# Rotary pairs swapped by transfers and copies instead of products in a three-layer hybrid block

## The chip, the core and the metric

The kernel runs on one core of a Trainium2 chip. Its engines work side by side, each through its own queue in order: TensorE (PE) for products, VectorE (DVE) and ScalarE (ACT) for work on tiles, GpSimd (POOL), and SyncE (SP), which here only issues the weights' transfers. They wait for each other through semaphores. The metric is the time of one execution in microseconds (us), measured on the device.

## What is computed

One sequence of 256 tokens with 1024 features goes through three layers, each a mixer and a gated feed-forward part (2816 wide), all in float32. The first layer mixes an RG-LRU, a gated linear attention and a block attention. The other two, which the change touches, mix an RWKV-7 recurrence, a dilated attention (B) and a latent attention (C):

```python
def rope_tables(positions, dim):
    inv_freq = 1.0 / (ROPE_THETA ** (jnp.arange(0, dim, 2, dtype=jnp.float32) / dim))
    ang = positions.astype(jnp.float32)[..., None] * inv_freq
    return jnp.cos(ang), jnp.sin(ang)

def apply_rope(t, cos, sin):
    t1, t2 = jnp.split(t, 2, axis=-1)
    c = cos[:, :, None, :].astype(t.dtype)
    s = sin[:, :, None, :].astype(t.dtype)
    return jnp.concatenate([t1 * c - t2 * s, t1 * s + t2 * c], axis=-1)

def partial_rope(t, cos, sin):
    rot, rest = jnp.split(t, [B_ROT_DIM], axis=-1)
    return jnp.concatenate([apply_rope(rot, cos, sin), rest], axis=-1)
...
    q = partial_rope(q, cos, sin)
    k = partial_rope(k, cos, sin)
...
    q = (rms_norm_2(cq, q_norm_g) @ w_uq).reshape(bsz, seq, C_HEADS, C_NOPE_DIM + C_ROPE_DIM)
    kv = (rms_norm_2(ckv, kv_norm_g) @ w_ukv).reshape(bsz, seq, C_HEADS, C_NOPE_DIM + C_V_DIM)
...
    q_rope = apply_rope(q_rope, cos, sin)
    k_rope = apply_rope(k_rope[:, :, None, :], cos, sin)[:, :, 0]
```

The first two calls are the dilated mixer's, on 16 of the 64 features of each of four heads (`B_ROT_DIM`); the last two are the latent mixer's, on 64 features of each query head and on one key that its four heads share. A rotation needs each feature beside its partner: 8 features away in B's heads, 32 in C's.

## The kernel before

Features lie on the 128 partitions and tokens along them, so a tile of two heads is 128 x 256. A feature's partner is on another partition.

Each float32 product is made of three: operands are split into a high part (`hi`, by ACT) and a rest (`lo`, by DVE), and `product` (line 466) runs hi by hi, lo by hi and hi by lo. The weights come in chunks of up to 1 MB through a ring of three buffers (`raw`, `w_hi`, `w_lo`): SP's queue loads a chunk, ACT writes `w_hi` (`hi_of`, line 1207), DVE `w_lo` (`lo_of`, line 1676). The order of all work on each engine is written out by hand; a step that others wait for is marked by name (`V.mark`, `A.mark`, `M.mark`) and awaited by that name.

In an RWKV layer (`rwkv(l)` on each engine) the recurrence needs the inverses of eight triangular 128 x 128 blocks, which are built up in levels n = 1 to 5 and a joining step 6. A level is: PE's first products (`inv_y`, line 937); ACT's copy of them (`inverse_y`); PE's back products (lines 921 and 926); DVE's subtractions from `x` and `xt` (line 1658), which the next level's first products wait for, half by half. DVE also makes masks for the level after (`level`, line 2158). Between and beside these steps each engine has `beside_inverse(n, half)`: half 0 stands behind the first products, half 1 behind the back products (on DVE: ahead of and behind the subtractions). What stands there:

- PE: at level 1 the projection of `bv` (chunk `in` 8, between the steps); at (2, 0) the products with `rot_b` for B's queries `bq` and keys `bk`, then `up(0)`; `up(1)`, `up(2)` at (2, 1), (3, 0); at (3, 1) the products with `dup` and `dup_rot`, which double C's shared rotary key `krope` from 64 to 128 partitions, plain and swapped, then `up(3)`; `up(4)` at (4, 0); at (4, 1) the product with `rot_c` for C's rotary queries `qr`; at (5, 0) the first attention scores; `up(5)`. `up(i)` are the products of the normed latents (`cq`, `ckv`) with `uq` and `ukv`.
- DVE: `rotate(n, dst, v, swapped, cos)` multiplies a tile by the cosine, its swapped copy by the sine and adds them: three operations. It rotates `bq`, `bk`, `krope` and `qr` at (2, 0), (3, 0), (3, 1) and (4, 1). `latents_lo` writes the latents' rests at (1, 1), behind it the evacuation of `bv` (line 1761), which `up(0)` waits for.
- ACT: copies of the latents into `h_hi` at level 1, copies of each `up(i)` (line 1451), and splits of chunks.

`cq_hi` and `cq_lo` are the first three tiles of `h_hi` and `h_lo`, which the projections read as their input until the last of them, that of `bv`, is done. So the copy waits for it (`act.wait_ge(M.sem, M.at(l, "in", 8))`). The swap matrices are constants with a sign in them, and the product's output stays in PSUM (banks 6 and 7).

Of the kernel before, what the change touches and what calls it, by code (L numbers as in the profile page):

```python
# [36 lines left out]
P = 128  # L37
# [96 lines left out]
def constants():  # L134
    i = np.arange(P)
    freq = np.zeros((P, 4), np.float32)
# [5 lines left out]
    freq[:, 2], freq[:, 3] = EPS, 64e-5  # L142

# [22 lines left out]
    rb, rc = np.zeros((P, P)), np.zeros((P, P))  # L166
    for h in (0, 64):
        for j in range(8):
            rb[h + j + 8, h + j], rb[h + j, h + j + 8] = -1, 1
        for j in range(32):  # L170
            rc[h + j + 32, h + j], rc[h + j, h + j + 32] = -1, 1
    dup = np.zeros((P, P))
    dup[i % 64, i] = 1
    out |= {"rot_b": rb, "rot_c": rc, "dup": dup}
    dupr = np.zeros((P, P))
    dupr[:64] = rc[:64, :64] @ dup[:64]
    out["dup_rot"] = dupr
# [49 lines left out]
def program(nc, ins, out, plan):  # L227


    with ExitStack() as ctx:  # L230
# [21 lines left out]
        rstd_col = sb("rstd_col", [P, TT])  # L252
        ARENA = 18752
        arena = sb("arena", [P, ARENA])
        bank = [ctx.enter_context(nc.psum_tensor(f"bank{i}", [P, 512], F32)) for i in range(8)]
# [70 lines left out]
        cq_hi, cq_lo = h_hi[:, 0:3, :], h_lo[:, 0:3, :]  # L326
        small = sb("small", [P, 96])
        filler = rope[:, 0, :]
# [15 lines left out]
        stored = sem("output_stored")  # L344
        V = Steps(sem("vector_step"), plan.get("V"))
# [100 lines left out]
        def _(pool):  # L446
# [13 lines left out]
        def _(pe):  # L460
# [602 lines left out]
            def up(l, i):  # L1063
# [8 lines left out]
                if i == 5:  # L1072
                    pe.wait_ge(V.sem, V.at(l, "rotated", 3))
# [13 lines left out]
            def beside_inverse(l, n, half):  # L1087


                b = AT2  # L1090
                if (n, half) == (2, 0):
                    pe.wait_ge(V.sem, V.at(l, "in", 7))
                    pe.wait_ge(A.sem, A.at(l, "rkv"))
                    pe.wait_ge(A.sem, A.at(l, "kb_turned"))
                    pe.matmul(bank[6][:, :], C("rot_b"), B2["bq"].rearrange("p a b -> p (a b)"), start=True, stop=True)
                    pe.matmul(bank[7][:, :], C("rot_b"), B2["bk"].rearrange("p a b -> p (a b)"), start=True, stop=True)\
                        .then_inc(M.sem, M.mark(l, "b_rot"))
# [7 lines left out]
                if (n, half) == (3, 1):  # L1105
                    pe.wait_ge(V.sem, V.at(l, "rotated", 0))
                    pe.matmul(bank[6][:, 0:T], C("dup")[0:64, :], B2["krope"][0:64, :], start=True, stop=True)
                    pe.matmul(bank[6][:, T:2 * T], C("dup_rot")[0:64, :], B2["krope"][0:64, :], start=True, stop=True)\
                        .then_inc(M.sem, M.mark(l, "k_rot"))
# [3 lines left out]
                if (n, half) == (4, 1):  # L1113
                    pe.wait_ge(V.sem, V.at(l, "rotated", 1))
                    pe.matmul(bank[7][:, :], C("rot_c"), b["qr"].rearrange("p a b -> p (a b)"), start=True, stop=True)\
                        .then_inc(M.sem, M.mark(l, "q_rot"))
# [86 lines left out]
        def _(act):  # L1203
# [105 lines left out]
            def ffn(l):  # L1309
# [21 lines left out]
                for p in range(1, FT // 2):  # L1331
# [4 lines left out]
                    if l == 0 and p == 6:  # L1336

                        act.wait_ge(V.sem, V.at("angles"))
                        for i in range(4):
                            last = act.activation(rope[:, i, :], rope[:, i, :], ACT.Sin)  # L1340
# [83 lines left out]
            def rwkv(l):  # L1424
# [6 lines left out]
                def beside_inverse(n):  # L1431
                    if n == 1:
                        hi_of(CHUNK[l, "ukv", 0])
                        act.wait_ge(M.sem, M.at(l, "in", 8))
# [1059 lines left out]
```

## Time and profile before

| | |
|---|---|
| median of 3 runs | 1014.27 us (1014.16 to 1014.28) |
| the profiled execution | 1013.86 us, span in the trace 1012.1 us |
| PE busy | 98% |
| DVE, ACT, POOL busy | 68%, 50%, 0% |
| granted TensorE clock | 0.999 |
| transfers | 156.41 MB, mean 155 GB/s |

The span runs from the first to the last instruction in the trace; the time of an execution is a little longer. Busy PE includes products that overlap, so a share of 98% says that it hardly ever waits, not that it is at its peak.

### The profile page before, as it was taken

The numbers are of one execution on the slowest core, as the hardware profiler recorded it, in microseconds if no ns is written. First come the engines' busy times: TensorE is split into PE (matmuls) and PEld (weight loads), VectorE is DVE, ScalarE is ACT, GpSimd is POOL, SyncE is SP. The second block draws the span as 40 slices with busy tenths as digits, with TensorE's granted clock in tenths as the row PEclk, the third lists the DMA queues.
The fourth block names the chain that finished last, engine by engine and source line by source line (L and its number), as shares of the span: only waits on it lengthen the run. The fifth ranks groups of instructions, "written<-read, shape, count | busy, mean of one in ns | idle before, by whom it ended". The sixth has DMA issues, their size and how long they took to land.

```text
span 1012.1 us, 20189 instructions
## 1 busy us (share of the span) xinstructions
PE 996.9 (98%) x8762; PEld 948.7 (94%) x8762; DVE 684.5 (68%) x1093; ACT 501.2 (50%) x667; POOL 3.0 (0%) x8
## 2 busy tenths in 40 slices
PE   9999999999999999999999999999999999999997
PEld 8898999999999889889999999999887999999997
DVE  6868586785656897856665565588877566565555
ACT  6466664435345652645544434375436364434433
POOL 0000000000000000000000000000000000000000
PEclk9999999999999999999999999999999999999999
DMA  9535345455544332314454545543231254555531
GB/s 332 179 113 200 138 147 190 173 209 186 189 170 159 109 111 85 124 46 141 167 208 174 196 173 180 196 161 116 79 111 44 89 203 170 189 184 173 202 126 42
DMA packets 24024, 156.41 MB, mean 155 GB/s; under 512 B 2608, under 2 KB 3936, under 8 KB 6400
## 3 DMA queue, kind: packets, MB, share of 16 engines
q1 hardware_dynamic: 21888, 151.70, 41.7%
q10 hardware_dynamic: 1840, 2.50, 0.7%
q8 instruction: 69, 1.13, 0.4%
q0 software_dynamic: 208, 0.92, 0.3%
q14 instruction: 19, 0.16, 0.0%
HBM read 154.05 MB, written 1.06 MB: 153 GB/s over the span
## 4 chain that ended last, share of the span: by engine, by line
PE 87%; DVE 6%; ACT 3%; issue 2%; DMA 1%; SPq 0%; ACTq 0%; DVEq 0%
PE bank L466 73%; DVE w_lo L1676 2%; ACT w_hi L1207 2%; DVE arena L1658 1%; PE bank L921 1%; PE bank L926 1%; PE bank L937 1%; DVE x L1658 1%; DMA x<-in_x 1%; PE bank L1145 1%; PE bank L1175 1%; DVE arena L2150 1%; DVE h_lo L1690 0%; ACT h_hi L1251 0%; PE bank L884 0%
## 5 line engine op out<-in xcount | busy, mean ns | idle before, releaser
L466 PE MATMUL bank<-h_hi,w_hi 128*128 128x256 f32 x1480 | 424.3, 287 | 3.7 <-DVE arena L1770 1.5
L1676 DVE TENSOR_TENSOR w_lo<-raw,w_hi 128x2048 fp32r<-128x2048 f32 (+2 forms) x142 | 318.7, 2250 | 155.9 <-ACT w_hi L1207 155.3
L466 PE MATMUL bank<-h_lo,w_hi 128*128 128x256 f32 x1480 | 418.7, 283 | 0.0
L466 PE MATMUL bank<-h_hi,w_lo 128*128 128x256 f32 x1480 | 418.6, 283 | 0.0
L1207 ACT ACTIVATE w_hi<-raw 128x2048 fp32r<-128x2048 f32 (+2 forms) x151 | 271.3, 1801 | 77.1 <-PE bank L466 74.9
L466 PEld LDWEIGHTS bank<-h_hi,w_hi 128*128 128x128 f32 x1480 | 283.6, 192 | 11.0 <-issue 4.9
L466 PEld LDWEIGHTS bank<-h_lo,w_hi 128*128 128x128 f32 x1480 | 283.7, 192 | 1.0 <-issue 0.7
L466 PEld LDWEIGHTS bank<-h_hi,w_lo 128*128 128x128 f32 x1480 | 283.7, 192 | 0.0
L466 PE MATMUL bank<-mix_hi,w_hi 128*128 128x256 f32 x720 | 207.0, 287 | 2.2 <-DVE mix_lo L1658 1.4
L466 PE MATMUL bank<-mix_lo,w_hi 128*128 128x256 f32 x720 | 203.7, 283 | 0.0
L466 PE MATMUL bank<-mix_hi,w_lo 128*128 128x256 f32 x720 | 203.7, 283 | 0.0
L466 PEld LDWEIGHTS bank<-mix_hi,w_hi 128*128 128x128 f32 x720 | 138.1, 192 | 5.1 <-DVE mix_lo L1658 2.3
L466 PEld LDWEIGHTS bank<-mix_lo,w_hi 128*128 128x128 f32 x720 | 138.1, 192 | 1.0 <-issue 1.0
L466 PEld LDWEIGHTS bank<-mix_hi,w_lo 128*128 128x128 f32 x720 | 138.1, 192 | 0.0
L1321 ACT ACTIVATE arena<-arena 128x256 f32<-128x256 f32 x66 | 27.6, 418 | 194.9 <-DVE arena L1658 194.9
L1658 DVE TENSOR_TENSOR arena<-arena 128x256 f32<-128x256 f32 (+2 forms) x134 | 71.6, 541 | 47.5 <-ACT arena L1321 35.3
L1207 ACT ACTIVATE arena<-bank 128x256 f32<-128x256 f32 (+3 forms) x72 | 30.9, 448 | 49.8 <-PE bank L603 17.2
L1658 DVE TENSOR_TENSOR mix_lo<-arena,mix_hi 128x256 fp32r<-128x256 f32 (+1 forms) x70 | 30.8, 441 | 33.3 <-ACT mix_hi L1207 33.3
L1207 ACT ACTIVATE mix_hi<-arena 128x256 fp32r<-128x256 f32 (+1 forms) x70 | 30.1, 430 | 38.5 <-DVE arena L1658 37.3
L1658 DVE TENSOR_TENSOR arena<-bank,rstd 128x512 f32<-128x512 f32 x66 | 45.1, 684 | 0.0
L466 PE MATMUL bank<-w_hi,h_hi 128*128 128x256 f32 (+1 forms) x84 | 25.7, 306 | 0.0
L1258 ACT ACTIVATE h_hi<-x,par 128x256 fp32r<-128x256 f32 x32 | 14.1, 500 | 22.6 <-DVE x L1658 16.5
(310 smaller groups left out, 844.3 us busy)
## 6 DMA issues: line engine op xcount, KB each, us to landing
raw<-in_w SPq DMA_DIRECT2D x136, 1024.0 KB, 4.8
raw<-in_w SPq DMA_DIRECT2D x5, 512.0 KB, 3.9
raw<-in_w SPq DMA_DIRECT2D x2, 896.0 KB, 4.4
raw<-in_w SPq DMA_DIRECT2D x2, 768.0 KB, 4.7
cst<-in_consts SPq DMA_DIRECT2D x1, 1184.0 KB, 10.6
arena<-bias_rows ACTq DMA_DIRECT2D x1, 1024.0 KB, 7.3
out<-arena ACTq DMA_DIRECT2D x4, 256.0 KB, 2.1
mat<-in_mat POOLq DMA_DIRECT2D x2, 384.0 KB, 3.4
```

The source lines that it names most:

```text
L466: last = pe.matmul(dst, w[a](k), act[b](k), start=start and i == 0 and j == 0, stop=stop and i == n - 1 and j == 2, skip_group_check=loose)
L921: last = pe.matmul(blocks(quads(2 + q)[h, m % 4, 0:64], n, 1), Y[h, m, :], blocks(XT[h, m, :], n, 1), start=True, stop=True)
L926: last = pe.matmul(blocks(quads(q)[h, m % 4, 0:64], n, 0), XT[h, m, :], blocks(Y[h, m, :], n, 0), start=True, stop=True)
L937: last = pe.matmul(quads(q)[h, m % 4, 0:64], BT[h, m, :], Xm[h, m, :], start=True, stop=True)
L1145: pe.matmul(dst(i), AT2["qn"][:, i - 4, queries], AT2["kn"][:, i - 4, keys], start=True, stop=False)
L1175: pe.matmul(dst(j), value(j, 0), att_p(l, j)[:, 0:T], start=True, stop=False)
L1207: return act.activation(dst, src, ACT.Copy, **kw)
L1258: last = act.activation(h_hi[:, k, :], x[:, k, :], ACT.Copy, scale=Par(g, k))
L1321: act.activation(FF["sg"][:, j % 2, :], FF["gu"][:, j % 2, 0, :], ACT.Silu)\
L1658: ins_ = dve.tensor_tensor(dst, a, b, op)
L1676: dve.tensor_tensor(w_lo[:, s, 0:n], raw[:, s, 0:n], w_hi[:, s, 0:n].bitcast(F32), ALU.subtract)\
L2150: last = dve.copy_predicated(gram[:, g, 2 * n:2 * n + 2, :].rearrange("p a b -> p (a b)"), mask, pairs(g % 4)[:, n, :])
```

## The change

The swap is no longer a product with a matrix. B's queries and keys: POOL issues four transfers each (8 partitions, two tiles of 256 columns, 16 KB) that move the partner features of two heads into another tile, `SWAP`. C's key: POOL copies it to the upper 64 partitions, then four copies of 32 partitions. C's queries: ACT writes the swapped tile with four more copies out of `up(2)`'s bank. The sign now sits in the sine tables, through a scale of -1 or 1 by partition in the sine (`freq`'s two new columns). The latents' parts lie in memory of their own, `latents`, over tiles of the area that are used later (`rs`, `nsa`, `s1`, `y`); so ACT's copy no longer waits for the last projection, and the memset of `s1` moves behind `up(2)`. The rotations stand one step sooner. DVE's split of chunk `out` 0 moves from (4, 0) to (3, 1), ACT's of `out` 1 behind `up(4)`.

```diff
+    freq[:, 4], freq[:, 5] = np.where(i % 16 < 8, -1, 1), np.where(i % 64 < 32, -1, 1)
...
+        latents = nc.alloc_sbuf_tensor_at("latents", [P, 2, 3, T], F32R, offset=arena_at + 29 * T * 4)
...
+        SWAP = dict(bq=B2["pm"][:, 0:2, :], bk=B2["pm"][:, 2:4, :], k=B2["pm"][:, 4, :], q=s_hl[:, 6:8, :])
+        HALF_PAIRS = [(slice(h + a, h + a + 32), slice(h + 32 - a, h + 64 - a)) for h in (0, 64) for a in (0, 32)]
+        cq_hi, cq_lo = latents[:, 0, :, :], latents[:, 1, :, :]
...
             for l in range(LAYERS):
+                if l:
+                    pool.wait_ge(V.sem, V.at(l, "kr"))
+                    for n, (dst, src) in enumerate(
+                            [(B2["krope"][64:P, :], B2["krope"][0:64, :])] +
+                            [(SWAP["k"][to, :], B2["krope"][from_.start % 64:from_.start % 64 + 32, :])
+                             for to, from_ in HALF_PAIRS]):
+                        if n:
+                            pool.wait_ge(k_swapped, 5 * l - 5 + n)
+                        pool.tensor_scalar(dst, src, 1.0, 0.0, ALU.mult, ALU.add).then_inc(k_swapped, 1)
+                    pool.wait_ge(M.sem, M.at(l, "gate"))
+                    for name, i in (("bq", 6), ("bk", 7)):
+                        pool.wait_ge(V.sem, V.at(l, "in", i))
+                        for h in (0, 64):
+                            for a in (0, 8):
+                                pool.dma_start(SWAP[name][h + a:h + a + 8, :, :],
+                                               B2[name][h + 8 - a:h + 16 - a, :, :]).then_inc(b_swapped[name], 16)
...
                 if (n, half) == (2, 0):
-                    pe.matmul(bank[6][:, :], C("rot_b"), B2["bq"].rearrange("p a b -> p (a b)"), start=True, stop=True)
-                    pe.matmul(bank[7][:, :], C("rot_b"), B2["bk"].rearrange("p a b -> p (a b)"), start=True, stop=True)\
-                        .then_inc(M.sem, M.mark(l, "b_rot"))
...
                 if (n, half) == (3, 1):
-                    pe.wait_ge(V.sem, V.at(l, "rotated", 0))
-                    pe.matmul(bank[6][:, 0:T], C("dup")[0:64, :], B2["krope"][0:64, :], start=True, stop=True)
-                    pe.matmul(bank[6][:, T:2 * T], C("dup_rot")[0:64, :], B2["krope"][0:64, :], start=True, stop=True)\
-                        .then_inc(M.sem, M.mark(l, "k_rot"))
                     up(l, 3)
...
-                if (n, half) == (4, 1):
-                    pe.wait_ge(V.sem, V.at(l, "rotated", 1))
-                    pe.matmul(bank[7][:, :], C("rot_c"), b["qr"].rearrange("p a b -> p (a b)"), start=True, stop=True)\
-                        .then_inc(M.sem, M.mark(l, "q_rot"))
...
                         hi_of(CHUNK[l, "ukv", 0])
-                        act.wait_ge(M.sem, M.at(l, "in", 8))
                         act.wait_ge(V.sem, V.at(l, "c_n"))
...
                         up(i)
-                        if i == 2:
+                        if i == 4:
                             hi_of(CHUNK[l, "out", 1])
...
+                    last = act.activation(up_to[i], up_bank(i), ACT.Copy, scale=scale if i < 3 else 1.0)
+                    if i == 2:
+                        for to, from_ in HALF_PAIRS:
+                            last = act.activation(SWAP["q"][to, :, :], up_bank(i)[from_, :, :], ACT.Copy, scale=scale)
+                    last.then_inc(A.sem, A.mark(l, "up", i))
...
                     if (n, half) == (1, 1):
                         latents_lo()
+                        dve.wait_ge(b_swapped["bq"], 64 * l)
+                        rotate(0, B2["bq"], B2["bq"], SWAP["bq"], 0)
                         evacuate(l, 8, B2["bv"], token_major=True)
-                    if (n, half) == (2, 0):
-                        after_m(l, "b_rot")
-                        rotate(0, B2["bq"], B2["bq"], pairs(6), 0)
                     if (n, half) == (2, 1):
                         lo_of(CHUNK[l, "ukv", 0])
+                    if (n, half) == (2, 0):
+                        dve.wait_ge(b_swapped["bk"], 64 * l)
+                        rotate(1, B2["bk"], B2["bk"], SWAP["bk"], 0)
                     if (n, half) == (3, 0):
-                        rotate(1, B2["bk"], B2["bk"], pairs(7), 0)
+                        dve.wait_ge(k_swapped, 5 * l)
+                        rotate(2, b["kro"], B2["krope"], SWAP["k"], 2)
                     if (n, half) == (3, 1):
-                        after_m(l, "k_rot")
-                        rotate(2, b["kro"], bank[6][:, 0:T], bank[6][:, T:2 * T], 2)
+                        lo_of(CHUNK[l, "out", 0])
                     if (n, half) == (4, 0):
-                        lo_of(CHUNK[l, "out", 0])
+                        after_a(l, "up", 2)
+                        rotate(3, b["qr"], b["qr"], SWAP["q"], 2)
+                        dve.nop().then_inc(V.sem, V.mark(l, "c_rope"))
                     if (n, half) == (4, 1):
-                        after_a(l, "up", 2)
-                        after_m(l, "q_rot")
-                        rotate(3, b["qr"], b["qr"], pairs(7), 2)
-                        dve.nop().then_inc(V.sem, V.mark(l, "c_rope"))
+                        after_m(l, "up", 2)
+                        dve.memset(B2["s1"].rearrange("p a b -> p (a b)"), 0.0)
```

The order on DVE, from the last subtraction of level 1 to the first of level 2, before (`h_lo` takes the latents' rests, `rstd_col` marks the evacuation of `bv`, `cst` the level masks, `rope` the tables):

```order
L1658 TENSOR_TENSOR arena<-arena,bank3 128x64x2
L1658 TENSOR_TENSOR h_lo<-spare_49,h_hi 128x512
L1658 TENSOR_TENSOR h_lo<-spare_49,h_hi 128x256
L1761 TENSOR_SCALAR arena<-bank4,rstd_col 128x256 x2
L2158 TENSOR_TENSOR arena<-arena,cst 128x256 x2
L1658 TENSOR_TENSOR spare_49<-arena,rope 128x512
L1658 TENSOR_TENSOR spare_49<-bank6,rope 128x512
L1658 TENSOR_TENSOR arena<-spare_49 128x512
L1658 TENSOR_TENSOR arena<-arena,bank0 128x32x4
```

and in the changed kernel:

```order
L1662 TENSOR_TENSOR arena<-arena,bank3 128x64x2
L1662 TENSOR_TENSOR latents_50<-spare_49,latents_50 128x512
L1662 TENSOR_TENSOR latents_50<-spare_49,latents_50 128x256
L1662 TENSOR_TENSOR spare_49<-arena,rope 128x512 x2
L1662 TENSOR_TENSOR arena<-spare_49 128x512
L1765 TENSOR_SCALAR arena<-bank4,rstd_col 128x256 x2
L2163 TENSOR_TENSOR arena<-arena,cst 128x256 x2
L1662 TENSOR_TENSOR spare_49<-arena,rope 128x512 x2
L1662 TENSOR_TENSOR arena<-spare_49 128x512
L1662 TENSOR_TENSOR arena<-arena,bank0 128x32x4
```

The rotation of `bq` has moved ahead of the evacuation, and that of `bk` has taken its place behind the masks; neither reads a bank.

The order on DVE from the last subtraction of level 3 to the first of level 4, before (`w_lo` is the split of chunk `out` 0):

```order
L1658 TENSOR_TENSOR arena<-arena,bank3 128x16x8
L1658 TENSOR_TENSOR spare_49<-bank6,rope 128x256 x2
L1658 TENSOR_TENSOR spare_49<-spare_49 128x256
L2158 TENSOR_TENSOR arena<-arena,cst 128x256 x2
L1676 TENSOR_TENSOR w_lo<-raw,w_hi 128x2048
L1658 TENSOR_TENSOR arena<-arena,bank0 128x8x16
```

and in the changed kernel, where the row ahead of the first subtraction is now the sum of `qr`'s rotation:

```order
L1662 TENSOR_TENSOR arena<-arena,bank3 128x16x8
L1680 TENSOR_TENSOR w_lo<-raw,w_hi 128x2048
L2163 TENSOR_TENSOR arena<-arena,cst 128x256 x2
L1662 TENSOR_TENSOR spare_49<-spare_49,rope 128x512 x2
L1662 TENSOR_TENSOR spare_49<-spare_49 128x512
L1662 TENSOR_TENSOR arena<-arena,bank0 128x8x16
```

The rotation of `krope` has left this stretch, that of `qr` has come in, and the split stands ahead of the masks.

The order on ACT from the copies of `up(0)` and `up(1)` on, before:

```order
L1451 ACTIVATE spare<-bank 128x512 x2
L1207 ACTIVATE w_hi<-raw 128x2048
L1207 ACTIVATE arena<-bank 128x256 x2
L1451 ACTIVATE spare<-bank 128x512
L1207 ACTIVATE w_hi<-raw 128x2048
L1451 ACTIVATE spare<-bank 128x512
L1207 ACTIVATE arena<-bank 128x256 x2
L1451 ACTIVATE spare<-bank 128x512
```

and in the changed kernel:

```order
L1452 ACTIVATE spare<-bank 128x512 x2
L1208 ACTIVATE w_hi<-raw 128x2048
L1208 ACTIVATE arena<-bank 128x256 x2
L1452 ACTIVATE spare<-bank 128x512
L1455 ACTIVATE spare<-bank 32x512 x4
L1452 ACTIVATE spare<-bank 128x512
L1208 ACTIVATE arena<-bank 128x256 x2
L1452 ACTIVATE spare<-bank 128x512
```

Behind `up(2)` stand four copies of 32 partitions instead of a `w_hi` split, which has moved behind `up(4)`.

## Rows read from the trace of the kernel before

**Rows 1.** The page, busy time of each engine and its share of the span

```profile
PE 996.9 (98%) x8762; PEld 948.7 (94%) x8762; DVE 684.5 (68%) x1093; ACT 501.2 (50%) x667; POOL 3.0 (0%) x8
```

**Rows 2.** The page, the chain that ended last, by engine

```profile
PE 87%; DVE 6%; ACT 3%; issue 2%; DMA 1%; SPq 0%; ACTq 0%; DVEq 0%
```

**Rows 3.** Line 1095 (`rot_b` by `bq`): ns min/median/max, first and last start

```profile
L1095 PE MATMUL bank<-arena,cst x4: 592/644/697, 398.4 to 737.5; 128*128 128x512 f32 x4
```

**Rows 4.** Timeline of PE, layer 1: start us, us, engine line

```profile
398.39 1.13 PE L1095 MATMUL bank<-arena,cst 128*128 128x512 f32 x2
...
400.42 0.36 PE L466 MATMUL bank<-h_hi,w_hi 128*128 128x256 f32 x1
...
408.47 0.66 PE L921 MATMUL bank<-arena 64*64 64x32 f32 x16
...
410.45 0.70 PE L1107 MATMUL bank<-arena,cst 64*128 64x256 f32 x2
...
411.51 0.39 PE L466 MATMUL bank<-h_hi,w_hi 128*128 128x256 f32 x1
...
412.41 1.15 PE L937 MATMUL bank<-arena 64*64 64x64 f32 x32
...
416.39 1.13 PE L1115 MATMUL bank<-spare,cst 128*128 128x512 f32 x2
417.44 1.15 PE L937 MATMUL bank<-arena 64*64 64x64 f32 x32
```

**Rows 5.** Timeline of DVE, layer 1; in brackets its idle time before, and the releaser

```profile
375.73 5.42 DVE L2150 COPY_PREDICATED arena<-cst,bank 128x256 f32<-128x256 uint32 x16 [0.80 <-PE bank L884]
...
388.21 0.69 DVE L1770 TENSOR_TENSOR arena<-bank,rstd 128x512 f32<-128x512 f32 x1 [0.82 <-PE bank L466]
...
394.36 0.49 DVE L1658 TENSOR_TENSOR arena<-arena,bank 128x128 f32<-128x128 f32 x2 [0.45 <-PE bank L926]
398.38 1.03 DVE L1658 TENSOR_TENSOR h_lo<-spare,h_hi 128x512 fp32r<-128x512 f32 x2 [3.54 <-ACT h_hi L1207]
399.45 0.88 DVE L1761 TENSOR_SCALAR arena<-bank,rstd_col 128x256 f32<-128x256 f32 x2
...
400.91 0.68 DVE L1658 TENSOR_TENSOR spare<-arena,rope 128x512 f32<-128x512 f32 x1
...
402.23 0.69 DVE L1658 TENSOR_TENSOR arena<-spare 128x512 f32<-128x512 f32 x1
...
410.57 0.49 DVE L1658 TENSOR_TENSOR arena<-arena,bank 128x128 f32<-128x128 f32 x2 [0.37 <-PE bank L926]
...
412.40 0.43 DVE L1658 TENSOR_TENSOR spare<-spare 128x256 f32<-128x256 f32 x1
413.22 0.82 DVE L2158 TENSOR_TENSOR arena<-arena,cst 128x256 f32<-128x256 f32 x2 [0.39 <-PE bank L937]
413.95 2.28 DVE L1676 TENSOR_TENSOR w_lo<-raw,w_hi 128x2048 fp32r<-128x2048 f32 x1
416.16 1.11 DVE L1658 TENSOR_TENSOR arena<-arena,bank 128x128 f32<-128x128 f32 x4
```

**Rows 6.** Timeline of ACT, layer 1; in brackets its idle time before, and the releaser

```profile
397.42 0.94 ACT L1207 ACTIVATE h_hi<-spare 128x512 fp32r<-128x512 f32 x2 [6.78 <-PE bank L466]
...
406.24 1.91 ACT L1207 ACTIVATE w_hi<-raw 128x2048 fp32r<-128x2048 f32 x1
408.04 0.65 ACT L1207 ACTIVATE arena<-bank 128x256 f32<-128x256 f32 x2
408.56 0.61 ACT L1451 ACTIVATE spare<-bank 128x512 f32<-128x512 f32 x1
```

**Rows 7.** Lines 448 and 453 on POOL: ns min/median/max, starts; its transfers' landing

```profile
L448 POOL TENSOR_SCALAR w_hi<-raw x1: 1038/1038/1038, 5.8 to 5.8; 128x1024 fp32r<-128x1024 f32 x1
...
L453 POOL DMA_DIRECT2D mat<-in_mat x2: 538/624/709, 114.4 to 461.7; - x2
...
DMA to landing us min/median/max: 3.3/3.4/3.6
```

More of the change, by code:

```diff
@@ L135, in constants @@
     i = np.arange(P)
-    freq = np.zeros((P, 4), np.float32)
+    freq = np.zeros((P, 6), np.float32)
     for h in (0, 64):
@@ L164, in constants @@
     out["dilated"] = np.where((dist >= 0) & (count > 0), np.log(np.maximum(count, 1)), NEG)
[L166 to L177, printed above, removed]
     return {k: np.asarray(v, np.float32) for k, v in out.items()}
@@ L251, in program @@
         rstd = sb("rstd", [P, T])
-        rstd_col = sb("rstd_col", [P, TT])
         ARENA = 18752
+        arena_at = nc.sbuf_base
         arena = sb("arena", [P, ARENA])
+        latents = nc.alloc_sbuf_tensor_at("latents", [P, 2, 3, T], F32R, offset=arena_at + 29 * T * 4)
         bank = [ctx.enter_context(nc.psum_tensor(f"bank{i}", [P, 512], F32)) for i in range(8)]
@@ L325, in program @@
             [B2[name].rearrange("p a b -> p (a b)")[:, 0:384] for name in ("kkn", "kp")]
-        cq_hi, cq_lo = h_hi[:, 0:3, :], h_lo[:, 0:3, :]
+        SWAP = dict(bq=B2["pm"][:, 0:2, :], bk=B2["pm"][:, 2:4, :], k=B2["pm"][:, 4, :], q=s_hl[:, 6:8, :])
+        HALF_PAIRS = [(slice(h + a, h + a + 32), slice(h + 32 - a, h + 64 - a)) for h in (0, 64) for a in (0, 32)]
+        cq_hi, cq_lo = latents[:, 0, :, :], latents[:, 1, :, :]
         small = sb("small", [P, 96])
+        rstd_col = sb("rstd_col", [P, TT])
         filler = rope[:, 0, :]
@@ L344, in program @@
         stored = sem("output_stored")
+        k_swapped = sem("k_rope_swapped_by_gpsimd")
+        b_swapped = {name: sem(f"{name}_pairs_swapped") for name in ("bq", "bk")}
         V = Steps(sem("vector_step"), plan.get("V"))
@@ L1071, in up @@
                     pe.wait_ge(A.sem, A.at(l, "up", i - 2))
-                if i == 5:
-                    pe.wait_ge(V.sem, V.at(l, "rotated", 3))
                 if i < 3:
@@ L1087, in beside_inverse @@
             def beside_inverse(l, n, half):
-                b = AT2
                 if (n, half) == (2, 0):
-                    pe.wait_ge(V.sem, V.at(l, "in", 7))
                     pe.wait_ge(A.sem, A.at(l, "rkv"))
                     pe.wait_ge(A.sem, A.at(l, "kb_turned"))
-                    pe.matmul(bank[6][:, :], C("rot_b"), B2["bq"].rearrange("p a b -> p (a b)"), start=True, stop=True)
-                    pe.matmul(bank[7][:, :], C("rot_b"), B2["bk"].rearrange("p a b -> p (a b)"), start=True, stop=True)\
-                        .then_inc(M.sem, M.mark(l, "b_rot"))
                     pe.wait_ge(V.sem, V.at(l, "c_lo"))
@@ L1339, in ffn @@
                         for i in range(4):
-                            last = act.activation(rope[:, i, :], rope[:, i, :], ACT.Sin)
+                            last = act.activation(rope[:, i, :], rope[:, i, :], ACT.Sin,
+                                                  scale=C("freq")[:, 4 + i // 2:5 + i // 2] if i % 2 else 1.0)
                         last.then_inc(A.sem, A.mark("rope"))
@@ L1450, in up @@
                     act.wait_ge(M.sem, M.at(l, "up", i))
-                    act.activation(up_to[i], up_bank(i), ACT.Copy, scale=scale if i < 3 else 1.0)\
-                        .then_inc(A.sem, A.mark(l, "up", i))
+                    last = act.activation(up_to[i], up_bank(i), ACT.Copy, scale=scale if i < 3 else 1.0)
[3 more added lines that the diff above has]
+                    last.then_inc(A.sem, A.mark(l, "up", i))
                 def inverse_y(n, q):
@@ L2140, in rwkv @@
                 gram = G2["gram"]
-                dve.memset(B2["s1"].rearrange("p a b -> p (a b)"), 0.0)
                 after_m(l, "v_turn")
```

## The prediction

> **What bounds the kernel now.** I read the page first: TensorE (PE) is busy for 996.9 of 1012.1 us [rows 1], and the chain that ended last is 87% PE [rows 2]. So only two things can move the end: less work in PE's queue, or a longer or shorter wait in it. The products that the change removes run once in each of the two RWKV layers; the two records of a line per layer, from 398.4 to 737.5 us, show both [rows 3]. I work the first out and double it. Next I read PE's timeline through the inverse, because the removed products stand between its levels [rows 4], then the engines that PE waits for there: VectorE (DVE) [rows 5], ScalarE (ACT) [rows 6], and GpSimd (POOL), which has almost nothing to do before [rows 7].
>
> What the reader is to see in these rows: PE issues without a gap, but the others are barely ahead of it. The `bv` evacuation starts at 399.45, takes 0.88 and ends at 400.33; PE's `up(0)` starts at 400.42. ACT's copy of Y for level 3 starts at 408.04, right behind a `w_hi` split of 1.91; PE's back products start at 408.47. DVE's subtractions of level 4 start at 416.16 and take 1.11; PE's level 5 starts at 417.44. A removed product is therefore worth its length only where these three are early too.
>
> **What is removed.** By starts in [rows 4]: the two `rot_b` products, 398.39 to 400.42, 2.03; the `dup` pair, 410.45 to 411.51, 1.06; `rot_c`, 416.39 to 417.44, 1.05. Together 4.14 a layer, 8.3 in all: the ceiling of the gain.
>
> **What each engine then allows**, in the time of layer 1:
>
> 1. Latents. Before, ACT's copy into `h_hi` waits 6.78 for the projection that reads it [rows 6], and DVE's `latents_lo` waits 3.54 for the copy [rows 5]. In other memory the copy needs only `c_n`, which DVE writes ahead of the level 1 subtractions, and 0.94 of ACT's time, which ACT has; so `latents_lo` can begin when DVE ends these subtractions, 394.36 + 0.49 = 394.85. It takes 399.45 - 398.38 = 1.07: 395.92.
>
> 2. `rotate(0)` follows, three operations of 512 columns, as before from 400.91 to 402.23 + 0.69 = 402.92: 2.01. The operand from PSUM and the one from SBUF are the same size and I cost them alike. It ends at 397.93, in time that DVE spent idle. The evacuation needs 0.88: 398.81; PE, free at 398.39, starts `up(0)` 0.09 behind it at 398.90 instead of 400.42. Gain 1.52; the other 0.51 of `rot_b` turns into a wait.
>
> 3. The transfers must be in time for that. POOL may start when `bq` is evacuated, 388.21 - 0.82 = 387.39 [rows 5]. A transfer holds POOL's queue 0.54 to 0.71 in the trace, and lands 3.3 to 3.6 after its issue, for a tile of 384 KB [rows 7]. These are 16 KB each, but no row has such a transfer. Lower bound: 0.54 each and nothing behind; upper: each waits for the one before, 3.4 each. I take 0.71 each and 3.4 behind the last issue, the nearest rows: four for `bq` by 387.4 + 2.9 + 3.4 = 393.7, needed at 395.9; eight by 387.4 + 5.7 + 3.4 = 396.5, `bk` needed at 399.6 (evacuation end 398.81 and the level masks behind it, 413.95 - 413.22 = 0.73). Hidden, with 2 to 3 us left.
>
> 4. Level 3. ACT's `up(1)` moves with PE by 1.52, the split of `out` 0 behind it and Y behind that: Y at 406.52, back products at 406.95 (408.47 - 1.52). `rotate(2)`, three operations of 0.43 or less [rows 5], some 1.2, falls into DVE's wait for these. PE then has no `dup` pair: level 4 starts at 412.41 - 1.52 - 1.06 = 409.83. DVE is in time: its last subtractions of level 3 end at 410.57 + 0.49 - 1.52 = 409.54. Gain so far 2.58.
>
> 5. Level 4, where the rest is lost. From 409.54 DVE has in a row the split of `out` 0 (416.16 - 413.95 = 2.21), the masks (0.73), `rotate(3)` (2.01) and the subtractions (1.11), 6.06 in sum: 415.6. PE, with `rot_c` gone, has done its back products at 416.39 - 2.58 = 413.81. It can issue the first half of level 5 when the first half of the subtractions is there, about 415.2, instead of 417.44. Gain 2.2 a layer: PE waits some 1.4 here, and of `rot_c` nothing is gained.
>
> 6. ACT. Four swap copies of 32 partitions and 512 columns join `up(2)`. No row has 32 partitions; a 128-partition copy of 512 columns takes 0.61 [rows 6], and four are 2.4 at most; if time went by partitions they would cost less, at least nothing. I take 0.55 each: Y ends at 406.52 + 0.65 = 407.2, `up(2)` and the swaps at about 409.8. That is before DVE wants them (409.54 + 2.21 + 0.73 = 412.5) and before PE does for `up(4)`, which stands behind the level 4 products that begin at 409.83. It is free because the 1.9 us split of `out` 1 moves behind `up(4)`. If the cover were gone, Y of level 4 would be up to 2.4 late.
>
> 7. POOL's copies of `krope`: 64x256, then four of 32x256, one behind the other. 128x1024 takes 1.04 [rows 7], so 0.26 by columns and perhaps 0.4 with the hand-over: some 2 us, from `kr` at about 371 to 373 or later, needed at 405. In their time DVE has a split running and then a wait of 0.80 before its masked copies [rows 5], so a small delay is absorbed.
>
> 8. The memset of `s1` (0.2 to 0.3) moves from ahead of that wait to behind the level 4 subtractions, where DVE waits for scores. The tables' sign is one operand of the sine. Both nothing. After level 6 the three engines all run 2.2 earlier and nothing else changes, so I carry the gain through.
>
> Sum: 2 x 2.2 = 4.4. The profiled execution took 1013.86 (span 1012.1 and 1.8 around it), the median of the runs is 1014.27, 0.4 above; 1014.3 - 4.4 = 1009.9.
>
> **The skill against this.** By rows, POOL's transfers land 2 to 3 us early [rows 7]. The Trainium skill, page "SBUF — State Buffer", section "A bandwidth-pool intuition that's wrong (but worth ruling out)", gives about 3.1 us for a transfer issued from GpSimd while VectorE holds a port that the two share, against 0.62 alone; by its figure eight in a row would be an estimated 25 us, `bk` near 412, and the kernel about 18 us slower. The same page, section "SBUF: two separate sides", says that a VectorE operation with two SBUF inputs and a GpSimd operation that reads SBUF shut each other out. No run here shows either; the first page rule stands beside the second rival below, the second beside the third.
>
> **The rivals.**
> - *Full gain*, 8.3: 1006.0. For it: PE is 98% busy. Against: steps 2 and 5 need DVE to be faster than its rows. If it is even a little, or PE's order hides more, 1006 to 1008.3. Chance 0.08.
> - *Transfers late*, slower. Mechanism: DVE's queue stands at the wait ahead of `rotate(0)` or `rotate(1)`, with the `bv` evacuation, the level masks and the subtractions behind it, so PE stands too. `bk` decides: beyond 399.6 there is 1.4 of slack (PE's `up(1)` covers level 2's subtractions) and 2.2 of gain to spend, so from (399.6 + 3.6 - 3.4 - 387.4) / 8 = 1.5 us a transfer the change loses. With one transfer at a time, 3.4 each, `bk` lands at 387.4 + 27.2 = 414.6, 15.0 late: 2 x (15.0 - 3.6) = 23 slower, 1037. For it: eight in a row were never issued; against: the 0.54 and 0.71 of rows 7. Chance of a loss over 0.2%: 0.08.
> - *Small thefts*: POOL's copies hold DVE up in the stretch where PE waits for its masked copies, or the four ACT copies run longer and push Y(4). Five copies at 0.35 less the 0.8 of idle time is 0.9 a layer, four ACT copies at 0.61 rather than 0.55 0.2: gain 2 x 1.1, 1012. Chance 0.17, half of it within 0.2%.
> - *Nothing moves*: the work goes to DVE, which bounds every level already. The rows speak against it (3.54 idle), 0.03.
>
> **How the numbers follow.** The forecast, a gain of 3.2 to 5.6 (1008.7 to 1011.1), has 0.64. The range leaves out the slow rival and most of the full gain and takes in the thefts: 1007.6 to 1012.8. 0.2% is 2.0 us, about what a measurement of this kernel can tell. Faster: 0.64 + 0.08 + 0.08 = 0.80; same: 0.11, from thefts and nothing; slower: 0.09.
>
> **What would show it.** In the new profile: `up(0)` 1.5 us closer to the end of level 2's first products; a wait of PE of about 0.5 for the `bv` evacuation and of about 1.4 for DVE's subtractions ahead of level 5; no wait of DVE for a transfer; DVE with no idle time from the level 3 subtractions to those of level 4; the last transfer's issue before 393.5 and its landing before 397 on this clock. The prediction is wrong if DVE waits for DMA, if a POOL copy or transfer lengthens a DVE operation, or if PE's wait at level 5 is 0 (then nearer 1008) or above 3.

## The result, and the profile after

The changed kernel takes 1017.8 us (median of 20 runs, 1012.72 to 1026.34), the kernel before beside it 1014.23 (20 runs, 1013.66 to 1014.39): a ratio of 1.0038, 95% interval 1.0022 to 1.0054 (ratios go by all runs and can differ from the quotient of the medians). It is slower, and the forecast of 1009.9 and its range are missed. The spread is the first thing to see. Before, 20 runs lie within 0.7 us, with a mean granted clock of TensorE of 0.999 in the profiled one. The 20 runs of the changed kernel fall into groups, and the clock falls with them: seven at 1012.7 to 1013.7 with 0.997, seven at 1017.5 to 1018.8 with 0.990 to 0.993, three at 1022.2 with 0.987 or 0.988, three at 1025.3 to 1026.3 with 0.983 or 0.984. The profiled execution took 1022.19 (span 1020.4), one of the third group.

The page of the changed kernel: busy times, and the granted clock in 40 slices, in tenths.

```profile
PE 999.1 (98%) x8742; PEld 952.8 (93%) x8742; DVE 685.0 (67%) x1093; ACT 507.3 (50%) x675; POOL 19.3 (2%) x34
...
PEclk9999999999999999699999999999999999999999
```

The 20 records fewer of PE are the ten removed products, with two records each [rows 3]; yet PE is busy 2.2 us longer than in [rows 1], and one slice of the clock, about 408 to 434 us, is a 6. Layer 1 there, on PE's timeline (to be laid beside [rows 4]; this trace is 0.4 later at level 1 than that of the kernel before):

```profile
397.72 1.15 PE L953 MATMUL bank<-arena 64*64 64x64 f32 x32
400.00 0.48 PE L482 MATMUL bank<-latents,w_hi 128*128 128x256 f32 x2 [1.14 <-DVE arena L1765]
...
414.36 0.63 PE L942 MATMUL bank<-arena 64*64 64x32 f32 x16
416.53 1.31 PE L953 MATMUL bank<-arena 64*64 64x64 f32 x32 [1.53 <-DVEq L2198]
417.77 1.32 PE L1141 MATMUL bank<-arena 64*128 64x256 f32 x8
419.02 1.06 PE L937 MATMUL bank<-arena 64*64 64x32 f32 x16
```

Two waits have taken the place of products, where the prediction put them: 1.14 for the `bv` evacuation (L1765) and 1.53 for DVE ahead of level 5. Level 5 starts at 416.53 instead of 417.44. The block of level 5 itself takes 1.31, as it also does behind a wait in runs that keep the clock (e1 below). But 2.5 us after the second wait a block of 16 small products takes 1.06, where the same form took 0.63 to 0.66 before the wait. The windows view gives the clock of the stretches (columns: window, its length, PE, PEld, DVE, ACT, POOL busy, granted clock, DMA share, GB/s):

```profile
395.00:418.00 23.00, 20.27 (x394) 18.85 (x394) 17.93 (x39) 11.33 (x19) 0.00 (x0) 1.00 0.37 133
418.00:438.50 20.50, 20.50 (x149) 15.23 (x147) 11.23 (x43) 7.95 (x25) 0.00 (x0) 0.50 0.15 52
438.50:460.00 21.50, 21.50 (x184) 17.46 (x185) 11.90 (x43) 10.69 (x29) 0.00 (x0) 1.00 0.14 46
...
762.00:766.00 4.00, 3.31 (x40) 2.85 (x40) 1.24 (x5) 0.77 (x2) 0.00 (x0) 0.61 0.35 147
```

For the 20.5 us from 418.0, 1.5 behind the start of level 5, the granted clock is 0.50, that is 1.2 GHz, the lower of its two levels, with PE busy the whole time; then it is 2.4 GHz again. In layer 2 the same wait, also 1.53, is followed by only some 3.5 us of it. POOL's load of `mat` in layer 2 waits for the first mixed chunk and marks when layer 1's attention is over: 461.67 before, 470.02 now.

DVE's timeline in the changed kernel (for [rows 5]):

```profile
394.77 0.49 DVE L1662 TENSOR_TENSOR arena<-arena,bank 128x128 f32<-128x128 f32 x2 [0.45 <-PE bank L942]
395.75 1.03 DVE L1662 TENSOR_TENSOR latents<-spare,latents 128x512 fp32r<-128x512 f32 x2 [0.50 <-DVEq L2198]
396.81 1.29 DVE L1662 TENSOR_TENSOR spare<-arena,rope 128x512 f32<-128x512 f32 x2
398.14 0.69 DVE L1662 TENSOR_TENSOR arena<-spare 128x512 f32<-128x512 f32 x1
398.87 0.88 DVE L1765 TENSOR_SCALAR arena<-bank,rstd_col 128x256 f32<-128x256 f32 x2
...
410.80 2.29 DVE L1680 TENSOR_TENSOR w_lo<-raw,w_hi 128x2048 fp32r<-128x2048 f32 x1
413.00 0.76 DVE L2163 TENSOR_TENSOR arena<-arena,cst 128x256 f32<-128x256 f32 x2
413.68 1.29 DVE L1662 TENSOR_TENSOR spare<-spare,rope 128x512 f32<-128x512 f32 x2
415.00 0.69 DVE L1662 TENSOR_TENSOR spare<-spare 128x512 f32<-128x512 f32 x1
415.84 1.12 DVE L1662 TENSOR_TENSOR arena<-arena,bank 128x128 f32<-128x128 f32 x4
```

POOL's eight transfers in its timeline, the line's total (ns min/median/max) and the landing times (for [rows 7]):

```profile
388.41 4.03 POOL L465 DMA_DIRECT2D arena<-arena  x8 [12.26 <-DVE arena L1772]
...
L465 POOL DMA_DIRECT2D arena<-arena x16: 499/506/561, 388.4 to 738.4; - x16
...
DMA to landing us min/median/max: 1.8/2.9/4.2
```

No DVE row waits for a transfer. The last of the eight is issued by 392.4, and even the slowest landing, 4.2, has them all there at 396.6, before the rotation of `bq` at 396.81. From 410.80 DVE stands on one row of work up to the subtractions of level 4, as forecast.

### The profile page after: what moved, and what is told of

The parts are those of the page before. It is cut to its first block and busy times, and to the rows that moved or that the text cites. A ratio compares the mean times of both kernels' runs of the same rounds, so it can differ in the third digit from the quotient of the medians.

```text
span 1020.4 us, 20181 instructions
## 1 busy us (share of the span) xinstructions
PE 999.1 (98%) x8742; PEld 952.8 (93%) x8742; DVE 685.0 (67%) x1093; ACT 507.3 (50%) x675; POOL 19.3 (2%) x34
## 3 DMA queue, kind: packets, MB, share of 16 engines
HBM read 153.79 MB, written 1.06 MB: 152 GB/s over the span
## 5 line engine op out<-in xcount | busy, mean ns | idle before, releaser
L482 PE MATMUL bank<-h_hi,w_hi 128*128 128x256 f32 x1448 | 414.3, 286 | 4.5 <-DVE h_lo L1694 1.6
L482 PE MATMUL bank<-h_lo,w_hi 128*128 128x256 f32 x1448 | 409.6, 283 | 0.0
L482 PE MATMUL bank<-h_hi,w_lo 128*128 128x256 f32 x1448 | 409.5, 283 | 0.0
L482 PEld LDWEIGHTS bank<-h_hi,w_hi 128*128 128x128 f32 x1448 | 277.5, 192 | 9.2 <-issue 4.3
L482 PEld LDWEIGHTS bank<-h_lo,w_hi 128*128 128x128 f32 x1448 | 277.6, 192 | 1.0 <-issue 0.7
L482 PEld LDWEIGHTS bank<-h_hi,w_lo 128*128 128x128 f32 x1448 | 277.6, 192 | 0.0
L482 PE MATMUL bank<-w_hi,h_hi 128*128 128x256 f32 x80 | 23.7, 297 | 0.0
```

Source lines behind the costliest of these rows:

```text
L482: last = pe.matmul(dst, w[a](k), act[b](k), start=start and i == 0 and j == 0, stop=stop and i == n - 1 and j == 2, skip_group_check=loose)
```

## The experiments

My theory at the start: the gaps in PE's work cost their length, and the one ahead of level 5 is followed by TensorE at half clock, which costs the rest. The rivals: the copies, transfers and waits cost by themselves what is missing, and the clock only accompanies it; or the new transfers and POOL's copies bring the fall about, and no wait of PE does. Below, "falls" are runs with a mean clock of 0.997 or less; the kernel before had none. This count is a lower bound. Every profiled execution, that of the kernel before too, ends with 0.8 to 4 us at half clock, so a mean of 0.998 can also hide a short fall in one layer; traces of e6 and e7 show that it did.

**e1_fill5.** The changed kernel with one product whose result nobody reads, in the gap ahead of level 5.

```diff
+                if (n, half) == (4, 1):
+                    pe.matmul(bank[7][:, :], cst[:, 0:P], cst[:, 0:512], start=True, stop=True)
```

> The changed kernel with one product of 512 columns (constants into bank 7, used by nobody) where the rot_c product stood at (4, 1), 1.05 us of PE's time twice. Theory A: PE's wait of 1.54 us ahead of the level 5 products is what TensorE's clock falls behind, to half. Then with the wait cut to about 0.5 the granted clock stays at 0.999 and the time no longer spreads: about 1011.5 (the changed kernel's lowest 1012.7 less one short fall in each layer), spread below 1 us. Rival B: the fall comes from the longer stretch, the wait of about 1 us for the bv evacuation counts as much: then the clock still falls in some runs and the spread remains, several us wide. Rival C: the fall has nothing to do with PE's waits (POOL's work or the transfers): unchanged, median 1018 and spread 13 us.

1011.61 (1011.11 to 1011.98, 9 runs), ratio 0.9976 (0.9966 to 0.9985); no falls. PE's timeline, and its window behind level 5:

```profile
414.96 1.12 PE L1119 MATMUL bank<-cst 128*128 128x512 f32 x2
416.56 1.31 PE L953 MATMUL bank<-arena 64*64 64x64 f32 x32 [0.48 <-DVEq L2200]
...
418.00:438.50 20.50, 20.50 (x237) 15.74 (x236) 15.96 (x66) 13.17 (x38) 0.00 (x0) 1.00 0.16 53
```

Level 5 starts at 416.56, as in the changed kernel (416.53); PE is given work to do that brings nothing, and the kernel is 6.2 us faster. In the same 20.5 us it gets 237 product records done instead of 149. So this is what the change is worth with the clock held, 2.5 us, and the rival in which the clock only accompanies the loss can't hold: copies and transfers are still there.

**e2_fill2.** The same product in the other gap, ahead of `up(0)`.

```diff
                     pe.wait_ge(A.sem, A.at(l, "kb_turned"))
+                    pe.matmul(bank[6][:, :], cst[:, 0:P], cst[:, 0:512], start=True, stop=True)
```

> The changed kernel with one idle product of 512 columns where the rot_b products stood at (2, 0), which covers PE's wait for the bv evacuation (1.13 and 0.78 us). The wait of 1.54 at level 5 stays. Theory A: no cure, median about 1018, spread 10 us or more. Rival B (both waits together): cured, about 1012.5 and spread below 1. Rival C: unchanged.

1018.35 (1016.9 to 1026.04, 6), ratio 1.0061 (1.0037 to 1.0085), falls in all 6. It is the gap ahead of level 5 that counts, and it is still there. The profiled execution (1017.83) has it in both layers:

```profile
416.68 1.66 PE L953 MATMUL bank<-arena 64*64 64x64 f32 x32 [1.53 <-DVEq L2199]
...
759.70 1.31 PE L953 MATMUL bank<-arena 64*64 64x64 f32 x32 [1.52 <-DVEq L2199]
```

In layer 1 the clock is at 0.50 from 417.5 to 431; in layer 2, behind 1.52, it stays at 1.00. So the same wait isn't followed by a fall every time.

**e3_before_wait5** and **e5_before_wait5_long.** The kernel before, with idle memsets on DVE behind the split of `out` 0, so that PE waits at level 5 as well: nothing of the change is in it. e3 has the two shown; e5 has the first of them twice, and each waits for the one before.

```diff
                         lo_of(CHUNK[l, "out", 0])
+                        dve.memset(s_m[:, 0:4, :].rearrange("p a t -> p (a t)"), 0.0)
...
+                        dve.memset(s_hl[:, 6:8, :].rearrange("p a t -> p (a t)"), 0.0)
```

> The kernel before, with two fills of zeros on DVE (1024 and 512 columns, some 1.6 us) behind the split of out 0 at (4, 0), so that PE waits about 1.5 us ahead of the level 5 products; nothing else of the change. By the wait alone 2 x 1.5 = 3.1 slower, 1017.3. Theory A: the clock falls behind this wait, runs spread over 5 us or more and the median is 1019 to 1025. Rival B (both waits together) and rival C (POOL or the transfers): clock 0.999, 1017.3 within 0.3 in all runs.

> The kernel before with three fills of zeros on DVE (1024, 1024, 512 columns, 2.4 us) behind the split of out 0 at (4, 0): the fills of the earlier run cost PE only 0.88 us of wait, so its wait never reached that of the changed kernel; these should make it about 1.8. All five removed products are still there, rot_c right ahead of the wait. By the wait alone: 1014.1 + 2 x 2.4 = 1019. Theory A (a wait above some 1.5 us at this place is enough): the clock falls, spread above 4 us, median 1022 or more. Theory D (it takes the wait and thin work ahead of it, which rot_c's wide product breaks up): clock 0.998 to 0.999, 1019 within 0.5.

e3 gave 1017.07 (1016.72 to 1017.48, 6), ratio 1.0029 (1.0018 to 1.0040), and no falls; but its wait was only 0.88, so it missed its dose and says little. e5 gave 1026.82 (1019.01 to 1033.5, 6), ratio 1.011 (1.0071 to 1.0149), with falls in 4 of 6. Its windows:

```profile
406.00:420.00 14.00, 11.76 (x227) 9.88 (x224) 11.05 (x22) 6.79 (x10) 0.00 (x0) 1.00 0.42 143
420.00:434.00 14.00, 14.00 (x139) 10.94 (x134) 9.11 (x30) 5.20 (x15) 0.00 (x0) 0.51 0.18 61
434.00:460.00 26.00, 26.00 (x220) 20.79 (x220) 15.88 (x60) 13.86 (x41) 0.00 (x0) 1.00 0.15 53
```

The run at 1020.47 with 0.998 may hide a fifth (the one at 1019.01 has 0.999). A wait of 2.19 alone, with no transfer, no copy on POOL, no latents in other memory and all products still there, brings the same half clock. The rival of transfers and POOL falls: a wait of PE is enough. It is longer than that of the changed kernel; one of 1.5 in the kernel before wasn't run.

**e6_before_norotc.** The kernel before without `rot_c` (the rotation of `qr` then reads what the bank held; this part of the computation is left out), and one memset on DVE.

> The kernel before without the rot_c product (the rotation of qr reads what is in bank 7, so C's queries are rotated with stale numbers: this part of the computation is left out), and one fill of 512 columns (0.5 us) on DVE at (4, 0). PE's wait ahead of level 5 should be 1.05 + 0.5 = about 1.6, with nothing wide ahead of it; rot_b and the dup pair are still there, POOL and the latents as before. By the wait alone: 1014.1 + 2 x 0.5 = 1015.1. Theories A and D: the clock falls in some or all runs, median 1018 or more, spread above 4. Rival C (POOL's work, transfers or the latents' place): 1015.1 within 0.5, clock 0.999.

1014.89 (1014.46 to 1020.58, 12), ratio 1.0018 (1.0006 to 1.0029). Its wait was 0.86, half of what was meant, and nearly that of e3; falls in 3 of 12, two of them at 1020.3 and 1020.6. The profiled execution isn't among the three, with 1015.67 and 0.998, but behind its wait in layer 2 stands a short fall, some 3.3 us at half clock:

```profile
756.00:758.00 2.00, 1.56 (x30) 1.59 (x32) 1.71 (x6) 0.38 (x1) 0.00 (x0) 0.61 0.75 217
758.00:760.00 2.00, 2.00 (x18) 1.49 (x17) 1.00 (x2) 0.38 (x1) 0.00 (x0) 0.53 0.77 320
```

A second run has the same time and clock, 1015.65 and 0.998, where the seven at 0.999 took 1015.0 or less. So it is 5 of 12, as the expectation of e10 has it. With `rot_c` ahead of the wait (e3) there were 0 in 6; so few runs don't separate the two.

**e7_fill5_wait.** e1's product, and a memset on DVE behind the split, so that the wait is as long as in the changed kernel though a wide product stands ahead of it.

```diff
                         lo_of(CHUNK[l, "out", 0])
+                        dve.memset(s_m[:, 0:4, :].rearrange("p a t -> p (a t)"), 0.0)\
+                            .then_inc(V.sem, V.mark(l, "pad", 0))
+                        after_v(l, "pad", 0)
```

> The changed kernel with the idle product where rot_c stood (as in the first run) and a fill of 1024 columns on DVE behind the split of out 0, 1.0 us, so that PE waits about 1.5 us ahead of level 5 again, now with a wide product in front of the wait. By the wait alone: 1011.6 + 2 x 1.0 = 1013.6. Theory A: the clock falls, spread above 4, median above 1017. Theory D: clock 0.998, 1013.6 within 0.5.

1015.65 (1014.08 to 1025.22, 12), ratio 1.0034 (1.0013 to 1.0054), a wait of 1.67, falls in 5 of 12. Four more runs, at 1015.2 to 1015.8 with 0.998, are apart from the three at 1014.1 to 1014.2 with 0.999. One of the four is the profiled execution (1015.28), and its layer 2 has such a fall:

```profile
755.00:760.00 5.00, 4.23 (x66) 3.75 (x68) 2.02 (x11) 0.77 (x2) 0.00 (x0) 0.66 0.06 23
```

So up to 9 of 12 lost the clock, four of them briefly, against 26 of 26 in the changed kernel and e2. The wide product may lower the odds; it doesn't take the danger away.

**e9_before_wait2.** e5's three memsets moved ahead of the `bv` evacuation, in the kernel before: a long wait at level 2, behind the wide products of `rot_b` and ahead of the `up` products.

> The kernel before with the three fills of the fifth run (1024, 1024, 512 columns, 2.4 us), now on DVE ahead of the bv evacuation at (1, 1): PE should wait some 2.2 us ahead of up(0), as long as it waited ahead of level 5 in the fifth run, where five of six runs lost the clock. Here the wait stands behind the projection of bv, level 2's first products and rot_b. By the wait alone 1014.1 + 2 x 2.3 = 1018.7. Theory A (length alone): the clock falls in most runs, median above 1022. Theory D (a wait costs the clock only where the work around it is thin): 1018.7 within 0.5 and clock 0.998 or more in every run.

1021.76 (1019.55 to 1025.47, 5), ratio 1.0071 (1.0057 to 1.0084), falls in 3 of 5 (a fourth run, at 1021.76, has 0.998). Its row of PE's waits (total, count, mean):

```profile
PE bank L466 <- DVE arena L1761: 5.7, 2, 2.8
```

and its windows behind that wait:

```profile
404.00:413.50 9.50, 9.50 (x108) 8.99 (x108) 4.18 (x10) 1.70 (x3) 0.00 (x0) 0.50 0.12 20
413.50:430.00 16.50, 16.50 (x319) 14.00 (x316) 13.20 (x37) 8.91 (x20) 0.00 (x0) 0.98 0.32 120
```

The narrower theory that I had formed by then, that only a wait among the small products of levels 4 and 5 matters, falls here. At level 2 the wait was 2.85; the 1.14 there in the changed kernel wasn't followed by a fall, and no length between was tried.

**e4_split_late.** The changed kernel with the cause of the wait taken away: the `w_lo` split of `out` 0 goes from ahead of the level 4 masks to behind the subtractions.

```diff
-                    if (n, half) == (3, 1):
-                        lo_of(CHUNK[l, "out", 0])
...
                         dve.memset(B2["s1"].rearrange("p a b -> p (a b)"), 0.0)
+                        lo_of(CHUNK[l, "out", 0])
```

> The changed kernel with DVE's split of out 0 moved from (3, 1) to behind the level 4 subtractions and the memset, (4, 1). DVE's row from the level 3 to the level 4 subtractions loses 2.2 us, so PE's wait ahead of level 5 should shrink from 1.54 to 0.1 to 0.5, with the wait of about 1 us at level 2 left. Theory A: clock 0.999, the level 5 products start 1.1 to 1.4 sooner a layer, so 1012.7 less about 1 for the short falls less 2.4: 1009 to 1010, spread below 1. Rival B: clock still falls in some runs. Rival C: 1015 with a spread of 13 us.

1010.10 (1010.01 to 1010.49, 5), ratio 0.9961 (0.9949 to 0.9973), wait at level 5 0.35, no falls.

**e10_late_wait09.** e4 with one memset ahead of the subtractions, for a wait between e4's and the changed kernel's.

> The kernel of the fourth run (the changed one with the split of out 0 late, PE's wait ahead of level 5 0.35 us, 1010.1) and a fill of 512 columns, 0.5 us, ahead of the level 4 subtractions: the wait grows to about 0.9, as in the third run (0.88 with rot_c ahead of it, no fall in 6) and the sixth (0.87 without rot_c but with rot_b and the dup pair, a fall of the clock in 5 of 12). Here all five products are gone. By the wait alone 1010.1 + 2 x 0.55 = 1011.2. If only rot_c's place counts: falls as often as in the sixth run, some 4 in 10. If the missing dup pair and rot_b count too: more often, most runs above 1012. If the sixth run's falls were something else: none.

1011.16 (1011.07 to 1011.84, 7), ratio 0.9972 (0.9961 to 0.9983), a wait of 0.71, no falls.

**e8_both_moved.** e4, and `latents_lo` moved from behind the last subtractions of level 1 to ahead of them, so that the other gap closes too.

```diff
                         lo_of(CHUNK[l, "uq", 0])
-                    if (n, half) == (1, 1):
                         latents_lo()
+                    if (n, half) == (1, 1):
```

> The changed kernel with the split of out 0 behind the level 4 subtractions (as in the fourth run, 1010.1) and latents_lo one step sooner, at the end of (1, 0), so that the rotation of bq starts 1.6 us sooner and the bv evacuation no longer waits for it. PE's wait at level 2 (1.13 and 0.78) should go to 0.1 or less, and the clock stay at 0.999. Gain over the fourth run 0.7 to 1.0 a layer unless ACT's row at level 3 takes it: 1008.3, by my range 1007.8 to 1009.3. If the wait at level 2 only moves (DVE's subtractions of level 1 come 1.1 later), 1010.1 as before.

1008.51 (1008.36 to 1008.53, 5), ratio 0.9944 (0.9932 to 0.9956), no falls: the best of all, 5.6 us faster than the kernel before beside it and 9.3 faster than the change. DVE's timeline:

```profile
392.77 1.02 DVE L1662 TENSOR_TENSOR latents<-spare,latents 128x512 fp32r<-128x512 f32 x2
...
397.76 0.88 DVE L1765 TENSOR_SCALAR arena<-bank,rstd_col 128x256 f32<-128x256 f32 x2 [0.37 <-PE bank L482]
```

PE's timeline, and the window that was at half clock in the changed kernel:

```profile
398.89 0.47 PE L482 MATMUL bank<-latents,w_hi 128*128 128x256 f32 x2 [0.17 <-ACT arena L1208]
...
414.23 1.31 PE L953 MATMUL bank<-arena 64*64 64x64 f32 x32 [0.35 <-DVEq L2197]
...
418.00:438.50 20.50, 20.36 (x195) 15.52 (x192) 16.55 (x71) 14.34 (x43) 0.00 (x0) 1.00 0.31 105
```

The evacuation now waits for PE and not PE for it, and level 5 starts 2.3 earlier than in the changed kernel, at full clock.

The waits at level 5 and what followed them, in order of length:

| kernel | wait, us | product of 512 columns just ahead | falls | and slower runs at 0.998 |
|---|---|---|---|---|
| e4, e8 | 0.35 | no | 0 of 10 | 0 |
| e1 | 0.48 | yes | 0 of 9 | 0 |
| e10 | 0.71 | no | 0 of 7 | 0 |
| e6 | 0.86 | no | 3 of 12 | 2 |
| e3 | 0.88 | yes | 0 of 6 | 0 |
| the change, e2 | 1.53 | no | 26 of 26 | 0 |
| e7 | 1.67 | yes | 5 of 12 | 4 |
| e5 | 2.19 | yes | 4 of 6 | 1 |

e1 to e4, e5 to e8, and e9 with e10 ran on three different chips; the kernel before took 1014.1 to 1014.2 on each.

## Why the prediction was wrong

**The transfers (step 3)** were right: hidden, at 0.51 of POOL's queue each, where 0.71 was taken, landing after 2.9 at the median, where 3.4 was. The rule of the Trainium skill that was set against them, some 3.1 us a transfer behind VectorE (page "SBUF — State Buffer", section "A bandwidth-pool intuition that's wrong (but worth ruling out)"), didn't show here; but its figure is for a `tensor_copy` of VectorE, and DVE's rows beside these transfers are all TENSOR_TENSOR and SCALAR_TENSOR_TENSOR, so this doesn't test it. The rival of late transfers is out.

**Latents and level 2 (steps 1, 2)** were right in kind and too generous. `latents_lo` began 0.98 behind the start of the last subtractions instead of 0.49; the 0.50 is a wait for a signal of DVE's own queue. The rotation took 2.06 from start to start instead of 2.01, and PE started 0.25 behind the evacuation's end instead of 0.09. PE's wait is 1.14 instead of 0.5 (0.8 in layer 2, where the 0.50 of DVE is missing). e8 shows the choice at stake: the same `latents_lo` fits ahead of the subtractions.

**Level 5 (step 5)**: the row of DVE's work was right item by item, and the wait of 1.53 is near the 1.4 forecast. Level 5 is 417.44 + 0.41 - 416.53 = 1.32 a layer earlier in step with the trace, instead of 2.2; the lack is that of step 2, 0.7, and some 0.2 more. Two layers make 2.6, less the 0.4 by which the trace is later from level 1 on (its cause is open): 2.2, which is the difference of the spans of before and e1 (1012.1 - 1009.9). The medians say 2.5. So the terms, with the clock held, would have given some 1011.7, inside the range, though the gain of 2.6 is short of the 3.2 to 5.6 called most likely.

**The step that failed** is the last of step 8, "After level 6 the three engines all run 2.2 earlier and nothing else changes, so I carry the gain through". Step 5 priced the wait at its length, and everything behind it at the durations of a trace whose clock was 0.999. A wait of 1.53 at this place was followed by TensorE at 1.2 GHz, in one layer or both, in 26 of 26 runs. That costs 1017.8 - 1011.6 = 6.2 at the median, and 1020.4 - 1009.9 = 10.5 in the two profiled executions, 9.1 of it in layer 1 (the load of `mat` at 470.02 against 460.94). A gain of 2.5 became a loss of 3.6. The Trainium skill says it in general, page "TensorE: Matmul & The Clock Gate", section "What's actually happening": the throttled state is the default, and activity lifts it. The traces agree in kind (0.50 behind the wait, 1.00 again later in the same busy stretch), though PE was busy through all 20.5 us at 0.50 before it was lifted. I had not weighed it: the granted clock is not among the signs that the prediction named, and of those that would have shown it wrong none came.

**ACT and POOL (steps 6, 7)**: four swap copies took 2.39 in a row, 0.59 each instead of 0.55, and Y and `up(2)` were still in time; the rival of small thefts had nothing to take here. POOL's five copies took 4.42 and not some 2, one of them 2.48, below; they hindered nobody.

**Shown and open.** Shown: closing the gap ahead of level 5, by a useless product (e1) or by moving its cause (e4), removes the falls; a wait alone brings them without any part of the change (e5, e9). Open: what decides in a given run whether the clock falls and for how long: behind the same wait of 1.53, 20.5 us in one layer and 3.5 in the other, and in e2 some 14 and none. Length moves the odds: with no wide product ahead, 0 of 17 at 0.35 to 0.71 and 26 of 26 at 1.53. That what PE did just before moves them too isn't shown: e7 differs from the change in length and chip as well, and e3 and e6 are too few.

## What to carry to other kernels

A product taken from a PE that is 98% busy is worth its length only where its inputs are early; else it leaves a gap, and a gap can cost several times its length in clock (here twice 1.53 us cost 6.2 at the median), so read the granted clock and the spread of the runs before looking for small thefts. One useless product in the gap is the test: if the kernel gets faster by doing more, it was the clock. The cure is to move the work that PE waits for, which here brought 4.0 us with the one gap (e4) where the useless product brought 2.5, and 5.6 with both gaps (e8).

## What the hardware showed beyond that

POOL's copies of `krope` in the changed kernel, line total and timeline row:

```profile
L459 POOL TENSOR_SCALAR arena<-arena x10: 398/401/2485, 371.7 to 722.2; 32x256 f32<-32x256 f32 x8, 64x256 f32<-64x256 f32 x2
371.73 4.42 POOL L459 TENSOR_SCALAR arena<-arena 64x256 f32<-64x256 f32 x5 [238.19 <-DVE arena L1662]
371.73 0.40 POOL L459 TENSOR_SCALAR arena<-arena 64x256 f32<-64x256 f32 x1 [238.19 <-DVE arena L1662]
372.21 2.48 POOL L459 TENSOR_SCALAR arena<-arena 32x256 f32<-32x256 f32 x1
```

and what DVE's timeline has beside them:

```profile
371.55 0.68 DVE L1774 TENSOR_TENSOR arena<-bank,rstd 128x512 f32<-128x512 f32 x1
372.15 2.28 DVE L1680 TENSOR_TENSOR w_lo<-raw,w_hi 128x2048 fp32r<-128x2048 f32 x1
374.65 0.69 DVE L1662 TENSOR_TENSOR arena<-bank,arena 128x512 f32<-128x512 f32 x1 [0.22 <-PE bank L890]
```

The second copy took 2.485 us, the others of this layer 0.40. It is the one that starts 0.06 behind DVE's split, an operation with two operands in SBUF, and it ends at 374.69, 0.26 behind the end of the split. The split keeps its 2.28, as in [rows 5]. The copies beside the other two rows, where one operand of DVE comes from a PSUM bank, take 0.40. Layer 2 repeats it: 2.474 for the second copy, 0.07 behind the start of a split. The Trainium skill has it so, page "SBUF — State Buffer", section "SBUF: two separate sides": an operation of VectorE with two SBUF inputs and one of GpSimd that reads SBUF exclude each other for a whole instruction. The trace agrees; no run here took it by itself. Two smaller ones: a copy by ACT of 32 partitions and 512 columns takes 0.59, about as much as one of 128 (0.60 to 0.61), and a POOL copy of 256 columns 0.40, not the 0.26 that columns alone would give.
